# SSD scan in a float32 two-layer block: outputs kept channel-major, both products of a chunk added in one PSUM bank, no transposes back

## The reference, cut to what matters

```python
cs = jnp.cumsum(a_dt, axis=2)                        # decay sums within a chunk
decay = jnp.where(causal, jnp.exp(cs_l - cs_s), 0.0)
cb = jnp.einsum('bclgn,bcsgn->bcgls', cc, bc)
y_diag = jnp.einsum('bcghls,bcsghp->bclghp', cb[:, :, :, None] * decay, xf)
states = jnp.einsum('bclgn,bclghp->bcghpn', bc, xf * jnp.exp(cs[:, :, -1:] - cs)[..., None])
# prev: the states carried over the chunks, h * exp(cs[:, :, -1]) + st
y_off = jnp.einsum('bclgn,bcghpn->bclghp', cc, prev) * jnp.exp(cs)[..., None]
y = y_diag + y_off + d_skip[:, None] * xs
y = y * silu(z);  y = groupnorm(y) * norm_w;  out = y @ w_out
```

## Time and profile before

| what | us |
|---|---|
| median of 3 runs | 3488.97 (3487.61 to 3493.29) |
| span of the profiled execution | 3490.1 |
| the four scans in it, first CB to the start of y(7) | 70.9, 82.7, 71.0, 67.9 |
| from the start of y(6) to the first product of the norm, group 0 and group 3 | 27.96, 15.06 |

### The profile page before, as it was taken

How to read it: one execution, slowest core, us unless ns; L and a number is a source line. 1 busy time by engine, 2 the same in 40 slices (tenths; PEclk the granted TensorE clock), 3 DMA queues, 4 the chain that set the end, 5 groups by cost and what they waited for, 6 DMA issues and landing times.

```text
span 3490.1 us, 38493 instructions
## 1 busy us (share of the span) xinstructions
PE 3246.4 (93%) x15304; PEld 2552.4 (73%) x15304; DVE 2050.2 (59%) x2723; ACT 1274.4 (37%) x1880; POOL 401.0 (11%) x436
## 2 busy tenths in 40 slices
PE   8988888999899999889999999898878989999998
PEld 7755565778677787567888887685566768888877
DVE  5555546555454545668777664676564677777334
ACT  2554425442433414463332323413424443323123
POOL 1001000020301203020000002340011310000012
PEclk9999999999999999989999999999988999999999
DMA  6210100212402121132223434422064332224233
GB/s 151 48 39 8 49 25 25 62 49 61 62 27 75 43 67 55 37 124 94 85 80 102 137 110 133 131 78 82 1 92 136 107 122 85 85 73 154 97 118 103
DMA packets 344883, 280.31 MB, mean 80 GB/s; under 512 B 52129, under 2 KB 313729, under 8 KB 344417
## 3 DMA queue, kind: packets, MB, share of 16 engines
q1 hardware_dynamic: 322480, 196.30, 19.7%
q0 software_dynamic: 22224, 81.56, 7.2%
HBM read 221.46 MB, written 52.82 MB: 79 GB/s over the span
## 4 chain that ended last, share of the span: by engine, by line
PE 72%; DVE 11%; ACT 7%; issue 5%; DMA 3%; POOL 1%; SPq 0%; ACTq 0%; DVEq 0%; POOLq 0%
PE PS L356 40%; PE PS L2186 12%; PE PA L2186 7%; PE PS L853 2%; PE PB L1602 2%; PE PA L864 1%; DVE WL L325 1%; DMA DEC<-ssd_decay_sums 1%; DVE XL L1865 1%; PE PA L396 1%; PE PB L876 1%; ACT PP L964 1%; DMA WS<-in_ffn_w_out_dram 1%; DVE XST L657 1%; PE PA L1596 1%
## 5 line engine op out<-in xcount | busy, mean ns | idle before, releaser
L356 PE MATMUL PS<-XH,WH 128*128 128x512 f32 x1744 | 613.5, 411 | 52.9 <-DVE WL L325 27.1
L356 PE MATMUL PS<-XL,WH 128*128 128x512 f32 x1744 | 585.0, 395 | 0.0
L356 PE MATMUL PS<-XH,WL 128*128 128x512 f32 x1744 | 583.1, 393 | 0.0
L318 ACT ACTIVATE WH<-WS 128x1024 fp32r<-128x1024 f32 (+1 forms) x235 | 231.8, 990 | 896.3 <-PE PS L356 855.2
L356 PEld LDWEIGHTS PS<-XH,WH 128*128 128x128 f32 x1744 | 331.6, 191 | 154.7 <-DVE WL L325 33.3
L356 PEld LDWEIGHTS PS<-XL,WH 128*128 128x128 f32 x1744 | 333.6, 191 | 71.3 <-issue 2.2
L356 PEld LDWEIGHTS PS<-XH,WL 128*128 128x128 f32 x1744 | 332.4, 191 | 70.9
L325 DVE TENSOR_TENSOR WL<-WS,WH 128x1024 fp32r<-128x1024 f32 (+1 forms) x235 | 272.4, 1160 | 190.2 <-ACT WH L318 189.9
L356 PE MATMUL PS<-TQH,WH 128*128 128x512 f32 x448 | 162.8, 398 | 9.0 <-DVE WL L325 8.3
L356 PE MATMUL PS<-TQL,WH 128*128 128x512 f32 x448 | 160.9, 394 | 0.0
L356 PE MATMUL PS<-TQH,WL 128*128 128x512 f32 x448 | 160.7, 393 | 0.0
(11 more groups left out here) (652 smaller groups left out, 6135.3 us busy)
## 6 DMA issues: line engine op xcount, KB each, us to landing
RAW<-in_ffn_w_in_dram SPq DMA_DIRECT2D x36, 1024.0 KB, 5.7
WS<-in_ffn_w_out_dram SPq DMA_DIRECT2D x48, 512.0 KB, 4.1
WS<-in_ssd_w_in_dram SPq DMA_DIRECT2D x40, 512.0 KB, 3.9
DEC<-ssd_decay_sums SPq DMA_DIRECT2D x32, 512.0 KB, 3.8
WS<-in_ffn_w_in_dram SPq DMA_DIRECT2D x32, 512.0 KB, 3.9
TQF<-ffn_hidden POOLq DMA_DIRECT2D x14, 1024.0 KB, 7.6
x_residual<-ACC POOLq DMA_DIRECT2D x6, 2048.0 KB, 7.8
WS<-in_w_mix_in_dram SPq DMA_DIRECT2D x22, 512.0 KB, 3.9
```

What stands on the lines that cost most here:

```text
L318: nc.scalar.activation(WH[:, s, 0:cols], WS[:, s, 0:cols], ACT.Copy).then_inc(W_HI[s], 1)
L356: last = nc.tensor.matmul(PS[s][0:width, c], w[:, s, k * width:(k + 1) * width], x[:, k, c], start=(k == 0 and j == 0), stop=(k == kt - 1 ...
```

## The change

The outputs of the scan stay channel-major, in `XST`, where x already lies. Two heads lie side by side on 128 partitions: each head's product writes 64 partitions. The stationary operand is now `XTOK` (64 columns) and the moving one `DEC`. The product with the carried state has `PREV` as stationary operand and, as moving one, `CDX`: C multiplied by the decays of each head. Both products are added up in one bank. The decays exp(cs) come by way of DRAM (`EC_D`) and are loaded, broadcast, by two DMAs of 256 KB for each chunk from 1 on (`ssd_load_decays`). DVE multiplies them by C (`ssd_decayed_c`). `ECS`, `YOS` and `SYT` are gone. ACT multiplies `XST` by the skip weight, four instructions of 1024 columns a group, ahead of the second chunk's exponentials; POOL did this before in eight parts. POOL decays `PREV` once y(c) has read it. The 32 transposes back are gone, and the first half block of the next group's first input goes into the last chunk. The four small loads in group 1 go behind POOL's last work of that group's chunks. The rows of the skip weight are loaded by two DMAs instead of one.

```diff
@@ ssd_load_decays, new (SP)
+        sp.wait_ge(SYD, TT * g + c)
+        for a in range(2):
+            r = c * SSD_HEADS + g * HPG + a * HPG // 2
+            src = EC_D[r:r + HPG // 2, :].rearrange("h l -> (h l)").unsqueeze(0).broadcast_to([P, HPG // 2 * P])
+            sp.dma_start(CDX[a][:].rearrange("p h l -> p (h l)"), src).then_inc(EC_IN[a], 16)
@@ ssd_sync
             for c in range(2, TT):
                 ssd_load_sums(sp, g, c)
+                ssd_load_decays(sp, g, c - 1)
                 if c % 2 == 0:
                     ssd_load(sp, *after[c // 2 - 1])
+            ssd_load_decays(sp, g, TT - 1)
@@ ssd_tensor
             ssd_scan_tensor(pe, g)
-            for f in range(4):
-                if f == 2 and ahead:
-                    ssd_in(pe, g + 1, 0, range(0, 4))
-                ssd_turn_back(pe, g, f)
             if ahead:
                 ssd_in(pe, g + 1, 0, range(4, KT))
@@ ssd_scan_tensor
             nc.tensor.matmul(PB[:, 0:P], BT[:, tok], CT[:, tok], start=True, stop=True).then_inc(SCB, 1)
-            if c:
-                pe.wait_ge(SPREV, 7 * g + c)
-                nc.tensor.matmul(PA[:, 0:GW], CT[:, tok], PREV[:], start=True, stop=True).then_inc(SYO, 1)
             if c < TT - 1:
                 pe.wait_ge(SXDD, 7 * g + c + 1)
-                nc.tensor.matmul(PA[:, HALF:HALF + GW], BTOK[:, c], XDD[c % 2][:], start=True, stop=True).then_inc(SST, 1)
+                if c >= 2:
+                    pe.wait_ge(SPREV, 7 * g + c - 1)
+                nc.tensor.matmul(PA[:, half(c % 2)], BTOK[:, c], XDD[c % 2][:], start=True, stop=True).then_inc(SST, 1)
                 ssd_gate_part(pe, g, c + 1)
-            pe.wait_ge(SMR, n + 1)
...
+            elif g + 1 < SSD_GROUPS:
+                ssd_in(pe, g + 1, 0, range(0, 4))
+            ssd_outputs(pe, g, c)
+
+    def ssd_outputs(pe, g, c):
+        n = TT * g + c
+        pe.wait_ge(SMR, n + 1)
+        if n:
+            pe.wait_ge(SYT_OK, n)
+        if c:
+            pe.wait_ge(SPREV, 7 * g + c)
+            pe.wait_ge(SCTE, 2 * (7 * g + c))
+        for f in range(4):
+            y = [PB[SSD_P * s:SSD_P * s + SSD_P, HALF + f * P:HALF + (f + 1) * P] for s in range(2)]
+            for s in range(2):
+                h = 2 * f + s
+                last = nc.tensor.matmul(y[s], XTOK[:, c, h * SSD_P:(h + 1) * SSD_P], DEC[n % 2][:, h], start=True, stop=(c == 0))
+            for s in range(2 if c else 0):
+                h = 2 * f + s
+                last = nc.tensor.matmul(y[s], PREV[:, h * SSD_P:(h + 1) * SSD_P], CDX[f // 2][:, h % 4], start=False, stop=True)
+        last.then_inc(SYD, 1)
@@ ssd_scalar
             ssd_decay(act, g, 0)
+            for f in range(4):
+                nc.scalar.activation(XST[:, f], XST[:, f], ACT.Copy, scale=vec("ssd_d", 4 * g + f)).then_inc(SSKIP, 1)
             for c in range(TT):
@@ ssd_vector
                 if c:
-                    ssd_add_diagonal(dve, g, c - 1)
...
+                    ssd_state(dve, g, c)
+                    ssd_add_skip(dve, g, c - 1)
+                    ssd_decayed_c(dve, g, c)
                 if c % 2 == 0:
                     b = SSD_AT[g, "z", c // 2]
                     split_lo(dve, b + 2, cols=cols_of(b + 2))
-            ssd_add_diagonal(dve, g, TT - 1)
+            ssd_add_skip(dve, g, TT - 1)
+            dve.wait_ge(SYT_OK, TT * g + TT)
             for f in range(4):
-                dve.wait_ge(SYTURN, 4 * g + f + 1)
-                v.tensor_tensor(ZT[:, f], ZT[:, f], PAB[f % 2][:], ALU.mult).then_inc(SGATED, 1)
+                v.tensor_tensor(ZT[:, f], ZT[:, f], XST[:, f], ALU.mult).then_inc(SGATED, 1)
@@ ssd_add_skip and ssd_decayed_c, new (DVE)
+        nc.vector.tensor_tensor(x, x, PB[:, HALF:].rearrange("p (f l) -> p f l", f=4), ALU.add).then_inc(SYT_OK, 1)
...
+        b = CT[:, c * P:(c + 1) * P].unsqueeze(1).broadcast_to([P, HPG // 2, P])
+        for a in range(2):
+            dve.wait_ge(EC_IN[a], 16 * (7 * g + c))
+            nc.vector.tensor_tensor(CDX[a][:], CDX[a][:], b, ALU.mult).then_inc(SCTE, 1)
@@ ssd_pool
             pool.wait_ge(SCOPY, 5 * g + 5)
-            if g == 1:
-                s5_rate_loads(pool)
...
                 if 0 < c < TT - 1:
-                    pool.wait_ge(SYO, 7 * g + c)
+                    pool.wait_ge(SYD, n + 1)
                     tt(heads(PREV[:]), heads(PREV[:]), of_group(CDEC, g, c), ALU.mult).then_inc(SPSC, 1)
-                tt(heads(SYT[:, c]), x, skip, ALU.mult).then_inc(SSK, 1)
+                if g == 1 and c == TT - 1:
+                    s5_rate_loads(pool)
```

More of the change, by code:

```diff
@@ L208, in _build @@
     PREV = at("PREV", 156, [P, GW])
-    YOS = at("YOS", 158, [P, GW])
+    CDX = [at(f"CDX{a}", 158 if a == 0 else 205, [P, HPG // 2, P]) for a in range(2)]
     ZT = at("ZT", 160, [P, 4, SEQ])
@@ L449, in vec_loads @@
             yield vec("ssd", 34 * g + 30, 4), rows(ins["ssd_norm"][0][g * GW:(g + 1) * GW])
-        for name, src in (("dtb", "ssd_dt_bias"), ("alog", "ssd_a_log"), ("ssd_d", "ssd_d")):
+        for name, src in (("dtb", "ssd_dt_bias"), ("alog", "ssd_a_log")):
             yield vec(name, 0, SSD_HEADS), ins[src].broadcast_to([P, SSD_HEADS])
+        skip = ins["ssd_d"].rearrange("o (q r) -> o r q", r=2)
+        for r in range(2):
+            yield vec("ssd_d", 0, SSD_HEADS // 2)[SSD_P * r:SSD_P * r + SSD_P], skip[:, r].broadcast_to([SSD_P, SSD_HEADS // 2])
     def vecs_sync(eng, n0, n1):
@@ L1438, in dt_scalar @@
             nc.scalar.activation(CSROW[:].rearrange("p a l -> p (a l)"), PB[:, HALF:HALF + 2 * P], ACT.Copy).then_inc(SMALL_A, 1)
-            for dst, src in ((ECS, PA[:, 0:N_DT]), (EDX, PA[:, HALF:HALF + N_DT]), (CDEC, PB[:, 0:N_DT])):
+            nc.scalar.activation(ECROW[:].rearrange("p a l -> p (a l)"), PB[:, HALF:HALF + 2 * P], ACT.Exp).then_inc(SMALL_A, 1)
+            for dst, src in ((EDX, PA[:, HALF:HALF + N_DT]), (CDEC, PB[:, 0:N_DT])):
                 nc.scalar.activation(dst[:].rearrange("p t h -> p (t h)"), src, ACT.Exp).then_inc(SMALL_A, 1)
@@ L1571, in ssd_turn @@
         last.then_inc(STURN, 1)
[L1573 to L1580, removed]
     def ssd_scan_tensor(pe, g):
@@ L1737, in ssd_conv, with ssd_state, ssd_add_skip, ssd_decayed_c @@
         split_lo(dve, b + 2, cols=cols_of(b + 2))
-    def ssd_add_diagonal(dve, g, c):
-        dve.wait_ge(SYD, TT * g + c + 1)
-        nc.vector.tensor_tensor(SYT[:, c], SYT[:, c], PB[:, HALF:HALF + GW], ALU.add).then_inc(SYT_OK, 1)
+    def ssd_state(dve, g, c):
+        dve.wait_ge(SST, 7 * g + c)
+        new = PA[:, half((c - 1) % 2)]
+        if c == 1:
+            nc.vector.tensor_copy(PREV[:], new).then_inc(SPREV, 1)
+        else:
+            dve.wait_ge(SPSC, 6 * g + c - 1)
+            nc.vector.tensor_tensor(PREV[:], PREV[:], new, ALU.add).then_inc(SPREV, 1)
+    def ssd_add_skip(dve, g, c):
+        x = XST[:, :, c * P:(c + 1) * P]
+        dve.wait_ge(SYD, TT * g + c + 1)
+        if c == 0:
+            dve.wait_ge(SSKIP, 4 * g + 4)
+        nc.vector.tensor_tensor(x, x, PB[:, HALF:].rearrange("p (f l) -> p f l", f=4), ALU.add).then_inc(SYT_OK, 1)
+    def ssd_decayed_c(dve, g, c):
+        b = CT[:, c * P:(c + 1) * P].unsqueeze(1).broadcast_to([P, HPG // 2, P])
+        for a in range(2):
+            dve.wait_ge(EC_IN[a], 16 * (7 * g + c))
+            nc.vector.tensor_tensor(CDX[a][:], CDX[a][:], b, ALU.mult).then_inc(SCTE, 1)
     def ssd_mask(pool, n):
@@ L1755, in ssd_pool @@
             pool.wait_ge(SCOPY, 5 * g + 5)
-            if g == 1:
-                s5_rate_loads(pool)
-            skip = vec("ssd_d", g * HPG, HPG).unsqueeze(2).broadcast_to([P, HPG, SSD_P])
+            if g == 0:
+                pool.wait_ge(EC_OUT, 16)
             for c in range(TT):
```

31 lines of the change are left out of this document (16 added, 15 removed).

## The result

In five runs each the kernel before took 3488.46 us (3485.72 to 3493.29) and the changed one 3500.72 us (3497.08 to 3509.82, all as medians with lowest and highest). The ratio is 1.0034, 95% interval 1.0023 to 1.0045: the change makes the kernel 0.34% slower. The forecast was 3494, in a range of 3470 to 3514, with slower as the likeliest of the three outcomes. The profiled execution has a span of 3499.1 us, 9.0 more than before; the ratio gives 12 us (8 to 16), so the two traces show a little less than the whole difference.

What follows compares the result with a forecast made beforehand. PE, busy 3246 of 3490.1 us, was taken to bound the kernel. Terms summed to -9.5, plus 15 for the clock: +5.5 on the span, carried to the median of 3488.97 as 3494 us, range 3470 to 3514.

Steps and rivals of the forecast that it cites:

- Outputs, -24.1: PE's output products up to y(6): 0.86 us less in each of seven chunks, four groups, -24.1 us.
- changes of tiling, +8.2: PE switching between full array and part of it: 41 uncovered changes of 0.2 us, +8.2 us.
- the last rival: Array halves don't overlap when both products add in one bank: y at 3.5 us, +52, 3546 us; chance 0.03.
- End of a group, -39.9: From y(6) to the norm: transposes go, half block covers y(7)'s operands; 13.3 us less in three groups, group 3 unchanged.
- Four small loads, -11.8: Group 1's scan: moved behind the last chunk, the loads no longer delay XDD and DEC; -11.8 us.
- POOL's wait, +42.8: Chunks 2 to 6: PREV's decay waits for y, XDD queues behind it, PE pauses; 20 x 2.14 us.
- The shared port, +9.2: Chunks 2 and 4: DVE's weight split comes between POOL's decay and XDD, making XDD 1.15 us later, eight times.
- the rival in which POOL keeps the port: POOL keeps the port or DVE's split comes after XDD starts, half clock seldom: 3470 to 3480 us; chance 0.27.
- ACT's multiplications, +6.1: Before chunk 1's exponentials: silu 1.8 us later, PE pauses before y(1) 1.1 in three groups, 2.8 in group 3.
- Clock, +15: Half clock on PE after the scans' new pauses: 3 of 12 short, 6 of 8 long, 1.7 us each.
- every pause costs the half clock: All 20 new pauses on PE bring the half clock: +25 us, 3514 us; chance 0.2.
- Loads of CDX: 1 MB follows y per chunk; second CDX multiplied at 8.5 us, needed at 10.5: covered only through POOL's pause.

Runs made afterwards that it cites:

- e1: Changed kernel, but POOL makes XDD of the next chunk before it waits for y to decay PREV: 3440.67 us, ratio 0.9854 to the kernel before.
- e6: Changed kernel, but POOL makes the next XDD before waiting for y, and ACT's skip multiplications follow its first silu and split: 3431.10 us, ratio 0.9828.
- e7: Changed kernel, but all output products of the array's first half precede those of the second, without taking turns: 3526.34 us, ratio 1.0102.
- e5: Changed kernel, but the four small loads stand again on POOL ahead of group 1's first XDD: 3511.67 us, ratio 1.0057.
- e3: Changed kernel, but DVE's weight split of chunks 2 and 4 is made one chunk later, behind CDX: 3488.15 us, ratio 0.9995.
- e2: Changed kernel, but ACT's four skip multiplications stand behind its first silu and split of a group: 3488.1 us, ratio 0.9982.
- e4: Changed kernel, but the next group's first half block stays behind y(7): 3523.35 us, ratio 1.0083.

## Why the prediction was right, term by term

The forecast's mechanism holds: pauses on POOL eat what the outputs and the ends give. With e1 they are gone and the same outputs and ends make the kernel 1.5% faster than before; no other single edit does that. The terms, against what the changed kernel and the experiments show:

- **Outputs, -24.1, and changes of tiling, +8.2.** 1.90 us from y to CB is the 1.74 + 0.2 of the forecast less 0.04, and a full-clock chunk by its terms is 9.2 - 0.86 + 0.2 + 2.14 = 10.7, as measured. In e6, where no pause covers the change behind y, a chunk without any wait is 8.65, 0.53 below before: 0.86 less two changes of 0.17. The state product comes 10.7 - 8.65 = 2.05 later in the changed kernel, where the forecast has 2.14. So each of the two terms is about 0.1 off per chunk, and they cancel. The prediction's comparison of 0.11 with 0.054 was of two forms, for its 0.11 is a full-array product of 64 columns; the like with like is e7, and it gives 0.11 too. Both products in one bank take turns as one product does, so the last rival is out.
- **End of a group, -39.9.** The ends are 12.7, 13.2 and 12.7 us shorter, -38.6, with the forecast's changes of tiling at -38.1. y(7) has no pause in groups 0 to 2. In group 3 the norm starts 15.1 us after y(6) (15.06 in the earlier trace rows), with the two waits that were forecast, here 4.71 and 4.31 us:
```profile
1397.37 0.70 PE L1620 MATMUL PB<-DEC,XTOK 128*64 128x128 f32 x4 [4.71 <-DVE CDX L1772]
...
1405.37 8.94 PE L396 MATMUL PA<-T,ONES 128*128 128x512 f32 x16 [4.31 <-DVE ZT L1723]
```
- **Four small loads, -11.8.** e5 gives 8 to 11 in the time and 12.8 in group 1's scan.
- **POOL's wait, +42.8.** 20 pauses, 5 in each group, as forecast. The state product starts 2.05 later than it would, as above; the idle time shown is 1.77, or 2.76 with the split in between, against some 2 and 3.2 in the forecast.
- **The shared port, +9.2.** 7 chunks instead of 8 (in group 3 chunk 4's split is of a smaller load, 0.69 us, and is over in time: 10.8), and 1.0 instead of 1.15: +7. e3 shows the cause. The Trainium skill (SBUF — State Buffer, Who interferes with whom) says that GpSimd and a VectorE instruction with two SBUF inputs exclude each other, and that the order of issue decides which of them blocks. The rows agree: the split (issued at 711.53) waited for `PREV` (711.48), and `XDD` (712.48) for the split. So the rival in which POOL keeps the port is out.
- **ACT's multiplications, +6.1.** Too low. ACT's timeline, group 0:
```profile
683.94 4.26 ACT L1645 ACTIVATE XST<-XST,VT 128x1024 f32<-128x1024 f32 x4
...
691.85 1.03 ACT L1652 ACTIVATE ZT<-PS 128x1024 f32<-128x1024 f32 x1
```
  The silu is 1.8 later than in the earlier trace rows, as forecast, and y(1) waits 1.31 where 1.1 was forecast. But this is group 0, which has the half clock at the scan's start and so gives ACT time. The step that failed is that groups 1 and 2 would have it too: they had not, and waited 2.92 and 3.05 as group 3 did (2.92, forecast 2.8). By the waits +10.2, with the clock behind them +12.3 by e2's trace. e6 showed that the 1.6 at c = 0 contained in it isn't ACT's, so 10.8 is left.
- **Clock, +15.** From c = 2 on 10 chunks have it at 1.6: +16. Of the short pauses 5 in 13 (forecast 3 in 12), of the long 5 in 7 (forecast 6 in 8). That this came so close is partly luck: e2, e4 and e5 have the same 20 pauses and show 8, 12 and 11 such chunks. The rival "every pause costs the half clock" is out. Its text has a slip: by its own numbers, -9.5 + 1.7 for each stretch, the sum passes +7 from 10 stretches on, not from 12.
- **Loads of CDX** are covered, as forecast. The prediction named waits for `CDX` as a sign that it is wrong, and five are there, but they are the forecast pauses before y(1) and before y(7) of group 3. DVE's own wait for a load plays a part only in the last (0.75 of the 4.71 us). That they are covered "only because of the pause on POOL" was too dark: without the pauses one load in e1 shows, by 0.4 us, and none in e6.

Summed: -17.7 (outputs, changes up to y(6)) - 38.6 - 12.8 + 42.8 + 7.0 + 10.8 + 16 = +7.5, against +8.1 between the two traces. The -17.7 and the 42.8 are the forecast's own values, since only their sum is measured in the changed kernel; the others are measured. The forecast of +5.5 on the span had the ACT term some 5 too low and the port 2 too high, so errors cancel in it. In the times the change costs 12 us by the ratio, where +5 was forecast. What stays open is which pauses the half clock follows: the same pause of 1.77 us has it in one chunk and not in the next.

## What to carry to other kernels

Before adding a wait to an engine's queue, list what stands behind it and who needs that next. Here a decay that waits for y cost 20 pauses only because the next `XDD` stood behind it, and making `XDD` first turned a loss of 0.34% into a gain of 1.5%. A wait named after a load or an operation may belong to what came late ahead of it on the same engine: y(1) "waits for `CDX`", and the cure was on ACT. Look at that engine's own idle time: with 7.65 us for the load in front (e5) it is the load, with none (e2, e6) it isn't. And price short pauses on PE with the clock: with 42.6 us of pauses 59 us of the span went.

## What the runs showed of the hardware

- The instructions of two products per place that add in one bank, on alternating halves of the array, start 0.054 us apart as those of single ones do; with neighbours on the same half 0.11 (e7).
- A change between the full array and halves of it cost about 0.17 us (8.65 us for a chunk in e6 with two of them).
- Behind pauses of 1.77 to 1.95 us in front of a state product the half clock came in 5 of 13 chunks; behind 2.76 us in 5 of 7. Each time it cost 1.6 us.
- POOL and DVE took turns by one instruction each: with `PREV` running, the split waiting and `XDD` next in POOL's queue, the order was `PREV`, split, `XDD` in 7 of 7 chunks with the long pause (2.76 us instead of 1.77).
- Four small loads issued by POOL ahead of its `XDD` held up loads of another queue: DVE waited 7.65 us for two of 256 KB (e5), and y(1) 7.32 instead of 2.92.
